# Order of splits, output parts, statistics and turned tiles in a four-layer kernel: four small reorderings

## What is computed

```python
def apply_partial_rope(x, cos, sin):   # angles from positions; used on q and k
    ...
for i in range(DEPTH):
    q, k, v = project_qkv(x, w_qkv[i], cos, sin)
    a = moba_attention(q, k, v) if i % 2 == 0 else sliding_window_attention(q, k, v, sinks[j])
    x = layer_norm(alpha * x + a.reshape(...) @ w_o[i], ln_mix_g[i], ln_mix_b[i])
    f = swiglu(x, ...) if i % 2 == 0 else moe_swiglu(x, ...)
    x = layer_norm(alpha * x + f, ln_ffn_g[i], ln_ffn_b[i])
    x = x + (p[i] @ w_ple_proj[i]) * jax.nn.sigmoid(x @ w_ple_gate[i])
...
# second block, layers 2 and 3
o_a = rmsnorm(gated_delta_rule(...)) * silu(z)
o_b = dilated_attention(rope(bq), rope(bk), bv)        # the local attention
mixed = jnp.concatenate([o_a, o_b], axis=-1) @ w_out
```

## Time and profile before

| | us |
|---|---|
| median of 3 runs | 2243.74 (2243.52 to 2244.27) |
| profiled execution, its time | 2243.76 |
| its span | 2242.0 |
| TensorE busy | 2177.8 (97%) |
| VectorE busy | 1699.2 (76%) |
| ScalarE busy | 1389.8 (62%) |
| mean granted TensorE clock | 0.992 of full |

### The profile page before, as it was taken

How to read it: one execution, slowest core, us unless ns; L and a number is a source line. 1 busy time by engine, 2 the same in 40 slices (tenths; PEclk the granted TensorE clock), 3 DMA queues, 4 the chain that set the end, 5 groups by cost and what they waited for, 6 DMA issues and landing times.

```text
span 2242.0 us, 32331 instructions
## 1 busy us (share of the span) xinstructions
PE 2177.8 (97%) x12316; PEld 1864.8 (83%) x12316; DVE 1699.2 (76%) x1876; ACT 1389.8 (62%) x1470; POOL 54.9 (2%) x72
## 2 busy tenths in 40 slices
PE   8899999889999999999999999989999999999998
PEld 6699997668888888888888887769979998988998
DVE  6745457768888888888888889867677777776766
ACT  5543334747777777777777777656465446565444
POOL 2000000010000000000000003000000000000000
PEclk9999999999999999999999999999999999999999
DMA  9655555359999999999999999844135554233551
GB/s 385 230 196 184 185 182 183 117 181 384 369 388 374 382 374 379 378 374 383 367 386 369 392 360 393 338 157 151 66 124 206 178 188 146 93 123 141 180 190 55
DMA packets 82234, 573.35 MB, mean 256 GB/s; under 512 B 9603, under 2 KB 9715, under 8 KB 16803
## 3 DMA queue, kind: packets, MB, share of 16 engines
q1 hardware_dynamic: 76752, 545.82, 64.4%
q0 software_dynamic: 5376, 26.12, 3.2%
HBM read 564.03 MB, written 17.83 MB: 260 GB/s over the span
## 4 chain that ended last, share of the span: by engine, by line
PE 86%; ACT 5%; DVE 5%; issue 2%; DMA 1%; SPq 0%; ACTq 0%; POOL 0%; DVEq 0%
PE bank L790 79%; ACT w_hi L527 2%; DVE w_lo L532 2%; PE bank L1095 1%; ACT arena L1430 1%; PE bank L1220 1%; PE bank L1230 1%; PE bank L1135 1%; DVE R L1937 0%; ACT L527 0%; PE bank L872 0%; PE bank L864 0%; DMA raw<-in_wu_qkv 0%; DVE arena L1950 0%; PE bank L765 0%
## 5 line engine op out<-in xcount | busy, mean ns | idle before, releaser
L532 DVE TENSOR_TENSOR w_lo<-raw,w_hi 128x2048 fp32r<-128x2048 f32 x506 | 1159.1, 2301 | 348.9 <-ACT w_hi L527 347.3
L527 ACT CAST w_hi<-raw 128x2048 fp32r<-128x2048 f32 x506 | 965.7, 1911 | 456.3 <-PE bank L790 453.6
L790 PE MATMUL bank<-w_hi,xT_hi 128*128 128x512 f32 x1184 | 472.4, 399 | 16.0 <-DVE w_lo L532 5.4
L790 PE MATMUL bank<-w_hi,xT_lo 128*128 128x512 f32 x1184 | 464.5, 392 | 0.0
L790 PE MATMUL bank<-w_lo,xT_hi 128*128 128x512 f32 x1184 | 464.1, 392 | 0.0
L790 PE MATMUL bank<-xT_hi,w_hi 128*128 128x256 f32 x1344 | 381.5, 284 | 7.1 <-DVE w_lo L532 3.9
L790 PE MATMUL bank<-xT_lo,w_hi 128*128 128x256 f32 x1344 | 381.0, 283 | 0.0
L790 PE MATMUL bank<-xT_hi,w_lo 128*128 128x256 f32 x1344 | 381.0, 283 | 0.0
L790 PE MATMUL bank<-w_hi,aT_hi 128*128 128x512 f32 x864 | 343.8, 398 | 3.2 <-DVE w_lo L532 3.2
L790 PE MATMUL bank<-w_lo,aT_hi 128*128 128x512 f32 x864 | 336.9, 390 | 0.0
L790 PE MATMUL bank<-w_hi,aT_lo 128*128 128x512 f32 x864 | 336.8, 390 | 0.0
(11 more groups left out here) (334 smaller groups left out, 1610.1 us busy)
## 6 DMA issues: line engine op xcount, KB each, us to landing
raw<-in_wu_eg SPq DMA_DIRECT2D x112, 1024.0 KB, 7.0
raw<-in_wu_eu SPq DMA_DIRECT2D x112, 1024.0 KB, 7.1
raw<-in_wu_ed SPq DMA_DIRECT2D x112, 1024.0 KB, 7.3
raw<-in_wu_up SPq DMA_DIRECT2D x44, 1024.0 KB, 4.8
raw<-in_wu_ffn_gu SPq DMA_DIRECT2D x28, 1024.0 KB, 4.9
raw<-in_wu_in SPq DMA_DIRECT2D x28, 1024.0 KB, 4.8
raw<-in_wu_down SPq DMA_DIRECT2D x22, 1024.0 KB, 4.9
raw<-in_wu_ffn_d SPq DMA_DIRECT2D x14, 1024.0 KB, 4.9
```

What stands on the lines that cost most here:

```text
L527: nc.scalar.copy(w_hi[:, place(i), :], src).then_inc(*E.hi.mark("unit", i))
L532: nc.vector.tensor_tensor(w_lo[:, place(i), :], raw[:, i % RAW, :], w_hi[:, place(i), :].bitcast(F32), ALU.subtract) \
L790: mm = nc.tensor.matmul(o, l[i], r[j], start=(first and n == 0), stop=(last and n == 2), skip_group_check=not lone)
```

## The change

It moves instructions and adds none. Four things:

1. At the start, ScalarE and VectorE split the fourth unit (`walk("qkv", 0, 4)`) right behind the third, ahead of the angles and of sine and cosine; the walk at the head of `mixer` is left for layer 1 only.
2. `out_projection` in layers 0 and 1: unit 2 (block 1, i = 0) is multiplied for both tiles ahead of `out_ready`. ScalarE does `walk("wo", L, 2)` ahead of tile 0's root and `walk("wo", L, 3)` ahead of tile 1's root. VectorE does `walk("wo", L, 2)` between tile 0's two halves, instead of behind both tiles' rests.
3. Layer 1's gate: VectorE takes the rests of tile 0 between the statistics of tile 1's halves (`tile_stats` becomes `half_stats`), and TensorE turns tile 1 behind one gate part instead of two.
4. `local_attention` on VectorE: `walk("in", L, 12)` moves from ahead of the first scores to behind the last `normalise`, ahead of the first `heads_rest`.

```diff
 def out_projection(L, late):
     part("wo", L, "wo", 1, aT, 2, 0, 0)
+    if L < 2:
+        part("wo", L, "wo", 1, aT, 2, 0, 1)
     out_ready(L, late)
     part("wo", L, "wo", 0, aT, 0, 1, 0)
     part("wo", L, "wo", 1, aT, 2, 1, 0)
-    part("wo", L, "wo", 1, aT, 2, 0, 1)
+    if L >= 2:
+        part("wo", L, "wo", 1, aT, 2, 0, 1)
     part("wo", L, "wo", 0, aT, 0, 1, 1)
     part("wo", L, "wo", 1, aT, 2, 1, 1)
...
 # embedding_gate, TensorE
     tile_ready(stage, 0, (0,))
     gate(0, 0, 0)
-    if L == 0:
-        turn_tile(stage, 1, ready)
+    turn_tile(stage, 1, ready)
     tile_ready(stage, 0, (1,))
     gate(0, 1, 0)
-    if L:
-        turn_tile(stage, 1, ready)
...
 # start, ScalarE (VectorE alike, ahead of consts and positions)
     for i in range(2, SPLIT):
         split_hi(M, ac, i)
+    walk("qkv", 0, 4)
     ac.wait_ge(*consts.at())
     ac.wait_ge(*angles.at("sin"))
...
 # mixer, ScalarE and VectorE
-    walk("qkv", L, 4)
+    if L:
+        walk("qkv", L, 4)
...
 # ScalarE, output projection
     walk("wo", L, 0)
+    walk("wo", L, 2)
     norm_root(L, "mix", 0)
-    walk("wo", L, 2)
     walk("wo", L, 1)
     copy_T((L, "mix"), L, 0)
+    walk("wo", L, 3)
     norm_root(L, "mix", 1)
-    walk("wo", L, 3)
     copy_T((L, "mix"), L, 1)
...
 # VectorE, local_attention
-    walk("in", L, 12)
     scores(L, 0)
     scores(L, 1)
     normalise(L, 0)
...
+        if i == 4:
+            walk("in", L, 12)
         if i >= 4:
             heads_rest(L, i - 4, 4)
         if i == 4:
             walk("in", L, 13)
...
 def norm_tile(L, which, v, t, take):
-    tile_stats(L, which, t, take)
+    half_stats(t, 0, take)
+    half_stats(t, 1, take)
     tile_normed(L, which, v, t)
-def tile_stats(L, which, t, take):
-    for nb in range(2):
-        take(t, nb)
-        step(V_.bn_stats(st6[:, t, nb, :], R[:, t, nb * 512:(nb + 1) * 512]))
+def half_stats(t, nb, take):
+    take(t, nb)
+    step(V_.bn_stats(st6[:, t, nb, :], R[:, t, nb * 512:(nb + 1) * 512]))
+def tile_normed(L, which, v, t):
     sync()
     V_.bn_aggr(...)
...
 # VectorE, output projection
     walk("wo", L, 0)
-    norm_tile(L, "mix", 4 * L, 0, take_wo)
+    half_stats(0, 0, take_wo)
+    walk("wo", L, 2)
+    half_stats(0, 1, take_wo)
+    tile_normed(L, "mix", 4 * L, 0)
     norm_tile(L, "mix", 4 * L, 1, take_wo)
     for t in range(NT):
         rest_T((L, "mix"), L, t)
-    walk("wo", L, 2)
     walk("wo", L, 1)
     walk("wo", L, 3)
...
 # VectorE, second norm of layer 1
     norm_tile(L, "ffn", 4 * L + 2, 0, take_rows)
-    tile_stats(L, "ffn", 1, take_rows)
+    half_stats(1, 0, take_rows)
     rest_T((L, "ffn"), L, 0)
+    half_stats(1, 1, take_rows)
     tile_normed(L, "ffn", 4 * L + 2, 1)
     rest_T((L, "ffn"), L, 1)
```

More of the change, by code:

```diff
@@ L2004, in norm_tile @@
             def norm_tile(L, which, v, t, take):
-                tile_stats(L, which, t, take)
+                half_stats(t, 0, take)
+                half_stats(t, 1, take)
                 tile_normed(L, which, v, t)
-            def tile_stats(L, which, t, take):
-                for nb in range(2):
-                    take(t, nb)
-                    step(V_.bn_stats(st6[:, t, nb, :], R[:, t, nb * 512:(nb + 1) * 512]))
+            def half_stats(t, nb, take):
+                take(t, nb)
+                step(V_.bn_stats(st6[:, t, nb, :], R[:, t, nb * 512:(nb + 1) * 512]))
+            def tile_normed(L, which, v, t):
                 sync()
                 V_.bn_aggr(mv[:, t, :], st6[:, t, :, :].rearrange("p a b -> p (a b)")).then_inc(*stats.mark(L, which, t))
-            def tile_normed(L, which, v, t):
                 ve.wait_ge(*stats.at(L, which, t))
```

## The result

| | before | after |
|---|---|---|
| median of 5 runs, us | 2243.74 | 2231.84 |
| lowest to highest | 2243.52 to 2246.16 | 2229.27 to 2236.39 |
| span of the profiled execution | 2242.0 | 2230.0 |
| TensorE busy | 2177.8 | 2174.8 |
| TensorE idle | 64.2 | 55.2 |

The ratio is 0.9946, with a 95% interval of 0.9934 to 0.9958. Forecast was 2231.2, with a range of 2227.0 to 2238.0. The profiled execution took 2231.84, 1.84 more than its span.

The account below looks back on a forecast made before the run. TensorE, busy 2177.8 of 2242.0 us, bounds the kernel; only its pauses or work can shrink. 4.7 + 3.95 + 0.7 + 1.9 + 1.3 = 12.6 us off 2243.76 gives 2231.2, range 2227.0 to 2238.0.

Parts of the forecast that it names:

- rival 1: At the start, the fourth unit lands late, so A gives only 1.9 us: 2234.0; chance 12%.
- rival 3: Splits only hold up tile 0's statistics and heads_rest: B in layer 0 gives 1, D 0; 2235.5 us; chance 12%.
- rival 4: Whole kernel slower, through ten more falls of the clock: 2246 us; chance 2%.
- B in layer 0: Output parts and splits: feed-forward 2.45 us earlier, plus 1.5 for the clock behind it; 3.95, bounds 1 and 4.1.
- D: Local attention, layers 2 and 3: scores 1.3 us earlier, 0.65 kept after a stall; 1.3 for both, bounds 0 and 1.3 per layer.
- the lower bounds: Least gain of each part, 1.9 + 1 + 0 + 1.0 + 0: together still 3.9 us, 2239.9.
- C: Layer 1's gate: first part starts 1.05 us earlier, pause of 1.03 ahead of tile 1's gone; 1.9, bounds 1.0 and 2.8.
- A: At the start, fourth unit's split ahead of the angles: keys turned at 30.9 instead of 35.68; 4.7 us, bounds 1.9 and 4.8.
- I take the 1.5 as won: Layer 0's feed-forward: the shorter pause of 1.4 us keeps the clock up behind it, worth 1.5.
- B, layer 1: Only the output parts' order counts: pause of 0.57 us ahead of 454.29 goes with its restart; 0.7, bounds 0 and 0.8.
- what is gained ahead of a stretch is passed on whole: Between edits TensorE bounds long stretches (experts, feed-forward) and its feeders wait for its readings, so earlier gains persist.
- Rival 2: Moved pauses may change clock level, some 1.5 us each; two falls more than forecast give 2234.2; chance 13%.

Follow-up runs that it names:

- after_again: The kernel after run once more, nothing edited: mean 2232.01 us over 5 executions, 2230.56 to 2235.04, ratio 0.9946.
- b_order: Kernel before with only TensorE's new order of the output parts, splits left where they were: 2240.32 us, ratio 0.9984.
- b_alone: Kernel before with the output parts' new order and both engines' moved `wo` splits, nothing else: 2238.72 us, ratio 0.9976.
- b_splits: Kernel before with only VectorE's and ScalarE's `wo` splits moved, output parts in the old order: 2243.77 us, ratio 0.9999.
- without_c: Kernel after with only layer 1's gate put back as it was: 2233.89 us, against 2231.98 for the kernel after.
- c_half: Kernel before with only VectorE's gate edit, rest of tile 0 between the halves of tile 1's statistics: 2243.94 us, ratio 0.9998.
- a_alone: Kernel before with only the fourth unit's split moved ahead of the angles: 2238.94 us, ratio 0.9975.
- d_alone: Kernel before with only output unit 2's split moved behind the last `normalise` of local attention, layers 2 and 3: 2242.66 us, ratio 0.9993.
- c_alone: Kernel before with only layer 1's two gate edits, VectorE's and TensorE's: 2243.97 us, ratio 0.9999.
- c_turn: Kernel before with only TensorE's gate edit, tile 1 turned behind one gate part: 2243.41 us, ratio 0.9996.

## Why the forecast held, point by point

Rivals 1, 3 and 4 of the forecast did not come: the fourth unit landed in time, B in layer 0 kept 3.96 and D 1.1 to 1.4 where rival 3 gives them 1 and 0, and of the lower bounds only C's was passed.

**A.** The fourth unit landed at 17.2, 0.4 ahead of the halfway value and far from rival 1's. Angles at 21.3, sine table at 23.22, rope at 25.45, the fifth unit's lo from 28.29, no wait behind the keys; each came 0.6 to 0.8 ahead of its forecast. 4.93 against 4.7, mean 4.6.

**B, layer 0.** 2.48 and 1.48 against 2.45 and 1.5. The output projection ended 0.75 earlier (0.8), the pause is 1.24 (1.4). (103.12, which the forecast calls the end of tile 1's rest, is its start; the sum uses it as the start and is right.) The step "I take the 1.5 as won" was right in six of seven executions with a short pause; after_again lost it at 98 to 104.

**B, layer 1.** 0.7 was right (0.70 to 0.74 where the clock held at 411, 0.2 to 0.35 where it fell). That only the parts' order counts is right too, since b_order alone has it. What failed is the bound "0 and 0.8", which ends at the router: 1.6 more came between router and gate (2.0 on average over the seven traces with the new order), where the low stretches of the selection and of the experts' start are shorter or gone. The forecast read no window there. Why the new order spares the second stretch, with the same pause ahead of it, the runs don't say.

**C.** The mis-sized term. Its pauses moved as forecast (0.99 at the first part, the 1.03 gone, 0.54 new), but of 1.9 nothing was left at the first scores of layer 2 in the profiled execution. From the gate's turn to layer 2's first projection it gained 2.70; then the clock fell at 1486 and at 1528, where it had not in the kernel before, and took 2.72 back. Over all traces without filling, the stretch gained 1.7 on average with both edits (3) and 0.5 without (7, the kernel before's 0 among them). The step that failed: "what is gained ahead of a stretch is passed on whole". It is, except where the gain itself is the clock's. From the gate's turn to layer 2's first projection, the six traces that gained 1.7 to 2.7 (b_alone, b_splits, without_c, c_half, after, after_again) all fell behind the pause of 2.40 that follows, at 1.04 to 1.09 for the fall; the three that gained 0.2 to 0.6 (b_order, a_alone, d_alone) and the kernel before kept their clock there. Three of those six have no edit of C, so most of their gain is the low stretch of the gate ending earlier. c_alone (3.44) and c_turn (2.85) had the gain and no fall; what decides, the runs don't say.

**D.** 0.70 to 0.71 per layer against 0.65, stall and all. In layer 2 of the kernel after only 0.42 was kept, which is not D's doing:

```profile
1627.59 0.88 PE L864 MATMUL bank<-cst,arena 128*128 128x128 f32 x6 [0.65 <-DVE arena L1952]
...
1630.29 0.84 PE L864 MATMUL bank<-cst,arena 128*128 128x128 f32 x6 [1.02 <-ACT arena L1442]
...
1636.14 0.66 PE L872 MATMUL bank<-arena 128*64 128x256 f32 x4 [0.59 <-DVE aT_lo L1958]
```

The 1.02 on ScalarE's copy stands in all six traces with part A, also where D is absent (a_alone lost 0.15 there), and in none of the eight without A.

**The sum.** Four parts alone gave 5.5 + 5.7 + 0.5 + 1.8 = 13.4 +- 1.4 in the mean times (the error of the kernel before enters four times), the whole 12.3 +- 0.7: additive within error. The forecast's 12.6 was close partly by luck. In the mean times A, B and D gave 0.8, 1.0 and 0.5 more than forecast and C 1.4 less, each within about two errors. In the trace C's missing 1.9 was made up by the 1.6 that B gave in a stretch which had no term. Rival 2 was the right one to name, and its price of 1.5 per fall was right (1.04 to 1.65, or 0 where a pause hides it). Against the forecast, three falls came in new places (411, 1486, 1528), the one at the experts' start went, and the low stretch of the gate is shorter.

## What to carry to other kernels

Moving a split or a half of a reduction to where the engine stands idle gave the removed pause, and the clock behind it, in A and in B, and about half of it in D, where the next wait took the rest. The consumer's order must be changed with it: alone, order and splits gave 0.6 and -0.9, together 4.0. A gain that is the clock's rather than a pause's should not be booked as permanent: run the same kernel twice, compare where the low stretches lie, and judge small edits by a stretch of the trace and by the mean of many executions together; the sum over one trace misled by 2.6 us for b_alone. Before filling a pause with matmuls, look up who still holds the bank they write: one pause was filled at no cost, in the other the filling itself waited 3.25 us.

## What the runs showed of the hardware that was not expected

- The two profiled executions of one program differ by 1.1 to 1.65 us in four of nine stretches and by 0.1 in total; single executions of the kernel after spread over 2229.3 to 2236.4.
- A fall of the clock costs nothing where its longer matmuls fill a pause that would come anyway (1.55 at 1859.83); near 1900, where none follows, it cost 1.56 to 1.65.
- Two filling calls in a pause of 2.40 us kept the clock at 1.00 in both kernels that had them, where without them it was 0.72 in the same 6 us (after, after_again). c_alone and c_turn kept it behind the same pause of 2.40 without filling, so two traces are little.
- ScalarE's copy of the second turned product starts 0.40 us behind the matmul that releases it in the kernel after, and 0.11 behind it in the kernel before, where nothing near it was changed; it goes with part A, far away in the program (0.40 in the six traces with it, 0.11 in the eight without). The cause is open and was not tried.
